# Two transformer blocks on one core: the order of the attention's steps, the two halves of a weight slab apart, and three smaller edits

## The reference

```python
# first block
mod = cond @ w_ada + b_ada                       # sh1, sc1, g1, sh2, sc2, g2, 1024 each
h = rms(x) * ln1_g * (1 + sc1) + sh1
fq, fk, fv, fg, dq, dk, dv = split(h @ w_in)
cum = cumsum(log_sigmoid(fg + b_f))              # forget gate, one per fox head and token
fox:  s = q.k / 8 + cum[t] - cum[s];  p = softmax(where(causal, s, -inf));  p @ v      # 8 heads
diff: p = softmax(q1.k1 / 8 + alibi) - lam * softmax(q2.k2 / 8 + alibi);    p @ v      # 4 heads
diff_out = rms(diff_out) * diff_norm_g * (1 - lam_init)
x = x + g1 * (concat(fox_out, diff_out) @ w_out)
h2 = rms(x) * ln2_g * (1 + sc2) + sh2
x = x + g2 * ((silu(h2 @ w_gate) * (h2 @ w_up)) @ w_down)
# second block: h @ w_in_2 (7 x 1024 columns), a spatial gating unit, 16 heads of causal attention with
# a bias by relative position, two gates, w_out_2, a squared-relu feed-forward, a per-layer gate, a last norm
```

## Time and profile before

| | us |
|---|---|
| median of 3 executions (lowest, highest) | 817.07 (816.53, 818.65) |
| the profiled execution, and its span | 818.92, 817.2 |
| PE busy | 775.0 (95%) |
| DVE busy | 466.4 (57%) |
| ACT busy | 390.6 (48%) |
| POOL busy | 59.4 (7%) |

### The profile page before, as it was taken

One profiled execution on the slowest core, in us unless ns is written; L12 is line 12 of the kernel. 1 busy time (PEld: TensorE's weight loads), 2 busy tenths in 40 slices (PEclk: granted clock), 3 DMA queues, 4 the chain that ended last, 5 costly groups with the idle time before them and its releaser, 6 DMA issues.

```text
span 817.2 us, 10224 instructions
## 1 busy us (share of the span) xinstructions
PE 775.0 (95%) x3955; PEld 616.8 (75%) x3955; DVE 466.4 (57%) x607; ACT 390.6 (48%) x544; POOL 59.4 (7%) x70
## 2 busy tenths in 40 slices
PE   3988899988999999999999999999999999999995
PEld 2667675656888889888878887777888888888884
DVE  3466676747565556464595436555565656545364
ACT  3255666644344334353634356665455545335252
POOL 2004030010000000000280000000010000000001
PEclk9999999999999999999999999999999999999998
DMA  9998336895655347656749464333565645564601
GB/s 275 289 361 274 112 105 254 312 397 195 219 194 184 125 155 232 232 180 203 255 162 331 155 205 154 105 104 111 170 194 162 200 156 201 164 201 154 206 26 51
DMA packets 86785, 158.73 MB, mean 194 GB/s; under 512 B 5226, under 2 KB 23875, under 8 KB 84690
## 3 DMA queue, kind: packets, MB, share of 16 engines
q1 hardware_dynamic: 84562, 151.16, 55.7%
q0 software_dynamic: 2128, 6.90, 2.7%
q10 hardware_dynamic: 48, 0.01, 0.0%
HBM read 156.99 MB, written 1.08 MB: 193 GB/s over the span
## 4 chain that ended last, share of the span: by engine, by line
PE 82%; DVE 5%; issue 3%; SPq 3%; ACT 3%; DMA 2%; POOL 1%; DVEq 0%; POOLq 0%; ACTq 0%
PE PS L872 25%; PE PS L874 24%; PE PS L873 24%; PE PS L986 3%; DMA raw<-in_w_ada 2%; PE PS L1066 1%; ACT whi L1165 1%; PE PS L960 1%; DVE wlo L1377 1%; PE PS L1037 1%; SPq L802 1%; PE PS L1092 1%; PE PS L1021 1%; SPq L790 1%; POOL hrs L1780 1%
## 5 line engine op out<-in xcount | busy, mean ns | idle before, releaser
L1377 DVE TENSOR_TENSOR wlo<-raw,whi 128x2048 fp32r<-128x2048 f32 (+1 forms) x126 | 280.2, 2226 | 190.4 <-ACT whi L1165 162.4
L1165 ACT ACTIVATE whi<-raw 128x2048 fp32r<-128x2048 f32 (+1 forms) x126 | 227.1, 1804 | 156.2 <-PE PS L874 156.2
L872 PE MATMUL PS<-whi,hT 128*128 128x512 f32 (+1 forms) x704 | 280.6, 399 | 2.2 <-issue 1.9
L874 PE MATMUL PS<-whi,hT 128*128 128x512 f32 (+1 forms) x704 | 272.8, 388 | 0.0
L873 PE MATMUL PS<-wlo,hT 128*128 128x512 f32 (+1 forms) x704 | 272.7, 387 | 0.0
L872 PEld LDWEIGHTS PS<-whi,hT 128*128 128x128 f32 x704 | 133.5, 190 | 33.1 <-issue 8.4
L874 PEld LDWEIGHTS PS<-whi,hT 128*128 128x128 f32 x704 | 133.3, 189 | 27.5
L873 PEld LDWEIGHTS PS<-wlo,hT 128*128 128x128 f32 x704 | 133.7, 190 | 23.9
L872 PE MATMUL PS<-whi,hidT 128*128 128x512 f32 x216 | 84.5, 391 | 0.0
L874 PE MATMUL PS<-whi,hidT 128*128 128x512 f32 x216 | 84.1, 389 | 0.0
L873 PE MATMUL PS<-wlo,hidT 128*128 128x512 f32 x216 | 84.1, 389 | 0.0
(11 more groups left out here) (227 smaller groups left out, 643.7 us busy)
## 6 DMA issues: line engine op xcount, KB each, us to landing
raw<-in_w_in SPq DMA_DIRECT2D x36, 1024.0 KB, 5.1
raw<-in_w_ff SPq DMA_DIRECT2D x32, 1024.0 KB, 5.2
raw<-in_w_ada SPq DMA_DIRECT2D x16, 1024.0 KB, 6.9
raw<-in_w_gate SPq DMA_DIRECT2D x10, 1024.0 KB, 5.4
raw<-in_w_up SPq DMA_DIRECT2D x10, 1024.0 KB, 5.1
raw<-in_w_down SPq DMA_DIRECT2D x10, 1024.0 KB, 5.2
raw<-in_w_ada SPq DMA_DIRECT2D x16, 512.0 KB, 7.2
raw<-in_w_out SPq DMA_DIRECT2D x8, 1024.0 KB, 5.1
```

The lines of the kernel that those rows point to most:

```text
L872: pe.matmul(o, ah, wh, start=(k == 0), stop=False)
L874: return pe.matmul(o, al, wh, start=False, stop=end)
L1165: act.activation(split_view(whi, i), slab_view(raw, slot, i), ACT.Copy).then_inc(hi_made, 1)
L1377: dve.tensor_tensor(split_view(wlo, i), slab_view(raw, slot, i), whole(split_view(whi, i)), ALU.subtract).then_inc(lo_made, 1)
```

## The change

1. **Row constant.** The fox heads' bias no longer has `cum[t]`: the step `cum` (two transposes, a copy) and, for each head, the two adds to `mcum` are gone; the bias is the mask alone.
2. **Attention.** `scores` is taken apart into `scores` (TensorE; maximum on VectorE), `exp` (ScalarE) and `probs` (VectorE's divisions). `heads u+2` follow right behind `scores u+1`, ahead of `exp` and `probs` of u+1.
3. **Slabs.** `split n` is now only the `whi` copy; `lower n` is the `wlo` subtraction. While pairs are worked on (`paired`), `lower` stands behind `probs`, or ahead of the slab's first piece if it has not come before; `split` stands behind `values`.
4. **Start.** `fgate` (forget gate) stands ahead of split 10, and `lam` is in two steps, the first in the start.
5. **Diff norm.** By two heads, the first two behind values 6; their turn stands ahead of `ada 18`.
6. **Norm 1.** `x` is no longer multiplied by the inverse root ahead of the transposes. VectorE makes a diagonal matrix of the inverse roots, and TensorE multiplies by it in place of the transpose (`first`, `turn`), tokens 0 to 127 first.

```diff
-BETWEEN = {"fox": (2, 1, 1, 2, 2), 1: (2, 1, 1, 2, 1), 2: (2, 1, 1, 1, 1), 3: (2, 0, 1, 1, 1),
+BETWEEN = {"fox": (3, 2, 1, 2), 1: (2, 2, 1, 2), 2: (2, 2, 1, 1), 3: (2, 1, 1, 1),
...
             if u != us[-1]:
                 out += [("scores", u + 1)]
+            if u + 2 <= us[-1]:
+                out += [("heads", u + 2)]
+            if u != us[-1]:
+                out += [("exp", u + 1), ("probs", u + 1)]
...
-            if u + 2 <= us[-1]:
-                out += [("heads", u + 2)]
...
+            if u == FOX_P + 2:
+                out += [("diffnorm", 0)]
+            if u == FOX_P + 3:
+                out += [("diffnorm", 1)] + turns("diff", 0, (0,))
...
-            order += {KC - 4: [("setup", 0)], KC - 3: early + [("relbias", 0)]}.get(j, [])
+            order += {KC - 4: [("setup", 0), ("lam", 0)], KC - 3: early + [("relbias", 0)]}.get(j, [])
...
-    order += early + [("fgate", 0), ("unit", 0), ("logf", 0), ("unit", 1)]
+    order += [("fgate", 0)] + early + [("unit", 0), ("logf", 0), ("unit", 1)]
     now = whole("fox", 2, "w_in", 2 * W, "h")
-    order += insert(now, (4, early), (5, [("cum", 0)]), (6, [("heads", 0)]))
+    order += insert(now, (4, early), (6, [("heads", 0)]))
...
         if it[0] == "piece" and it[1]["first"] and it[1]["slab"] >= KC + 2:
-            while split <= min(it[1]["slab"] + min(2, it[1]["slab"] + 1), len(slabs) - 1):
-                out.append(("split", split))
-                split += 1
+            held = tiles[it[1]["T"]]["name"] == "w_out" and it[1]["k"] == 4 and tiles[it[1]["T"]]["n"] == 1
+            split = up_to("split", split, max(wanted, it[1]["slab"] + 1))
+            wanted = it[1]["slab"] + (2 if held else 3)
+            if not paired:
+                split = up_to("split", split, wanted)
+            lower = up_to("lower", lower, it[1]["slab"] + 1 if paired else split)
         out.append(it)
+        if it[0] == "scores":
+            paired = it[1] not in (FOX_P + DIFF_P - 1, PAIRS - 1)
+        if it[0] == "probs":
+            lower = up_to("lower", lower, split)
+        if it[0] == "values":
+            split = up_to("split", split, wanted)
...
+                elif kind == "first":
...
+                    for c in range(2):
+                        k = 2 * i + c
+                        pe.matmul(PS[:, b, c * S:c * S + P], x[:, 0, k * P:(k + 1) * P], diag[:, 0, :], start=True, stop=True)
...
-                            dve.tensor_scalar(mcum[:, a % 2, 0:P], mask[:, P:2 * P], cumq[:, 0, a:a + 1], None, ALU.add)
...
-                            bias = [mcum[:, a % 2, c0:c1] for c0, c1 in QB]
+                            bias = [mask[:, P:2 * P], mask]
...
+                elif kind == "norm" and i == 1:
+                    for t in range(TB):
+                        dve.wait_ge(rs1_made, t + 1)
+                        dve.tensor_scalar(diag[:, t, :], ident, nrs[:, 1, t:t + 1], None, ALU.mult).then_inc(diag_made, 1)
```

More of the change, by code:

```diff
@@ L203, in plan @@
     tail += insert(fill, *[(j, [ada[10 + j]] + ([("grow", 0)] if j == 5 else [])) for j in range(8)])
-    order += [("scores", 0), ("heads", 1), ("lam", 0)] + tail[:3]
+    order += [("scores", 0), ("heads", 1), ("exp", 0), ("probs", 0)] + tail[:3]
     tail = tail[3:]
     order += attention(list(range(FOX_P + DIFF_P)), tail, ada[18:20])
-    order += [("diffnorm", 0)] + ada[20:21] + turns("diff", 0, (0, 1)) + ada[21:22]
-    order += slab(wo[0], "w_out", 0, 4) + [("evac", wo[0])]
+    order += ada[20:22] + turns("diff", 0, (1,)) + insert(slab(wo[0], "w_out", 0, 4), (2, [("mod", 1)])) + [("evac", wo[0])]
     order += insert(slab(wo[1], "w_out", W, 4), (1, [("sums", (1, 0))])) + [("evac", wo[1]), ("sums", (1, 1))] + ada[22:24]
-    order += [("mod", 2), ("norm", 1)]
-    order += turns("norm", 1, (0, 1)) + parts("norm", 1, (0, 1)) + turns("norm", 1, (2, 3)) + parts("norm", 1, (2, 3))
+    order += [("norm", 1), ("first", 0), ("mod", 2), ("first", 1)]
+    order += turns("norm", 1, (0, 1)) + parts("norm", 1, (0, 1)) + [("first", 2), ("first", 3)]
+    order += turns("norm", 1, (2, 3)) + [("split", None)] + parts("norm", 1, (2, 3))
     late = []
@@ L230, in plan @@
                 m = FOX_P + DIFF_P
-                now = insert(now, (0, [("heads", m)]), (3, [("scores", m), ("heads", m + 1)]))
+                now = insert(now, (0, [("heads", m)]), (3, [("scores", m), ("heads", m + 1), ("exp", m), ("probs", m)]))
             order += now
@@ L982, in _ @@
                         pe.wait_ge(s, v)
-                    for c in range(2):
-                        for t in range(TB):
-                            o = c * S + t * P
-                            last = pe.transpose(PS[:, b, o:o + P], src[:, t, c * P:(c + 1) * P], ident)
+                    if is_affine(i):
+                        for c in range(2):
+                            last = pe.matmul(PS[:, b, c * S + P:(c + 1) * S], src[:, 1, c * P:(c + 1) * P], diag[:, 1, :],
+                                             start=True, stop=True)
+                    else:
+                        for c in range(2):
+                            for t in range(TB):
+                                o = c * S + t * P
+                                last = pe.transpose(PS[:, b, o:o + P], src[:, t, c * P:(c + 1) * P], ident)
                     last.then_inc(turned, 1)
@@ L1001, in _ @@
                     reader[6] = [(cum_made, 1)]
-                elif kind == "cum":
-                    take(5)
-                    pe.wait_ge(cum_made, 1)
-                    for t in range(TB):
-                        last = pe.transpose(PS[:, 5, t * FOX:(t + 1) * FOX], fgt[0:FOX, 3, t * P:(t + 1) * P],
-                                            ident[0:FOX, 0:FOX])
-                    last.then_inc(cumq_ps, 1)
-                    reader[5] = [(cumq_in, 1)]
                 elif kind == "heads":
@@ L1371, in _ @@
                 kind, i = it
-                if kind == "split":
-                    slot = landed(dve, it)
+                if kind == "lower":
+                    slot = landed(dve, ("split", i))
                     dve.wait_ge(hi_made, i + 1)
@@ L1444, in _ @@
                     last.then_inc(lam_dot, 1)
+                elif kind == "lam":
                     dve.wait_ge(lam_exp, 1)
@@ L1811, in _ @@
                     n = i
+                    if n == 1:
+                        for t in range(TB):
+                            pool.wait_ge(sums_made, 3 + t)
+                            then(pool.tensor_tensor(nss[:, 1, t:t + 1, 0], nss[:, 1, t:t + 1, 0], nss[:, 1, t:t + 1, 1], ALU.add))
+                            last = inverse_root(nrs[:, 1, t:t + 1], nss[:, 1, t:t + 1, 0], D)
+                            last.then_inc(rs1_made, 1)
+                        continue
                     if n:
```

123 lines of the change are left out of this document (64 added, 59 removed).

## The result

The changed kernel takes **873.33 us** (median of 4 runs, 872.39 to 873.54) where the kernel before, on the same chip, takes 817.86: ratio 1.068 (1.066 to 1.070). The forecast was 847 with a range to 857. The sign and the late low halves of the first block came out as forecast; behind the first block's gate products 19.4 us more were lost than forecast, most of it in the second block's attention.

A forecast was written before the change was run, and what follows sets the result against it. TensorE, busy 775.0 of 817.2 us, was taken as the bound. Terms 4.2 + 1.9 + 4.8 + 4.4 + 9.0 + 3.3 − 1.1 + 3.6 = +30 on 818.9 gave 849, by the median 847 us; range 829 to 857.

The forecast's parts named there:

- slab 12: First block: its low half stands behind the hss reduction, so it starts 5.4 us late, plus 1.7 of slow clock.
- Slab 13: First block: its low half stands behind probs 2, so TensorE waits 4.6 us, plus 1.7 of slow clock.
- Heads 0: Start of attention: wait for the second `unit` leaves a gap of 5.75 us, with 1.7 of slow clock +7.4.
- heads 4: First block, behind scores 3: needs `unit 3`, ready at 135.2 but wanted at 132.3, +2.9 us.
- Slabs 15 and 16: First block: low halves late behind probs, +1.7 us for slab 15 and +3.05 for slab 16.
- the strict queue: SP queue: slab 18's transfer waits for lower 16 and delays `ada 11` behind it, +3.5 us and 1.7 clock.
- the sum for MoBA: Second block's attention: waits of 2.2 us go, lower 77 costs 3.85 and 1.7 clock, other low halves in time; net +3.6.
- the price of the clock: TensorE: every gap over about 2 us costs its length and 1.7 us more at half speed.
- rival 1: Stalls only: low halves late, but the clock holds or the queue is not late; 835 to 837, both 826; chance 0.24.
- norm 1: Gate: scaling and its wait go, sixteen diagonal products cost 1.7 us extra, lower 21 costs 0.5; net −1.1 us.
- the faster one: VectorE makes low halves 12, 13 and 16 in time, so only removed waits count: 17 us less, 800; chance 0.05.
- Worse: Late low halves delay later transfers further, each another 1 to 2 us through `ada` chunks: 858 to 865; chance 0.06.

The follow-up runs named there:

- back_first: The changed kernel with the second block's low halves placed behind `back` on VectorE instead of ahead of it: 854.51 us, ratio 1.046.
- heads_back: start_back with heads u+2 between the probability transposes again, as in the kernel before: 815.52 us, ratio 0.996.
- start_back: The changed kernel with both slab halves at one place, forget gate behind split 10 and `lam` behind pair 0's divisions again: 820.20 us, ratio 1.002.
- best4: heads_back with pair 0's exponentials and divisions ahead of heads 1, and heads 0 one piece later: 810.71 us, ratio 0.991.

## Why the prediction was right in one half and wrong in the other

**Right: the low half is the loss, and slab 12 decides.** "Slab 12 can start about 5.4 us after slab 11's last matmul": it was 5.20, at 104.64. Slab 13: 4.6 forecast, 4.31 measured. Heads 0: 5.75 and 5.52; heads 4: 2.9 and 2.91; ada 11: 3.5 and 3.91. Slabs 15 and 16 were over-sized: 1.7 and 3.05, measured 1.03 and 1.98. With both halves at one place (822 us) all waits for slabs and transfers are gone, and their places alone bring most of the loss into the kernel before (859.5 us), so the cause is shown.

**Right: the strict queue.** With slab 18's transfer behind it, `ada 11` waits 2.8 us less; up to the gate about 1.9 of it stay gained. All the ada waits were forecast as 8.8 us and are 10.7. The 7.1 us of the earlier trace rows was no measure of this stretch: from 155 to 210 us a transfer of ada weights takes 10.5 to land, at the median of 13.

**Wrong: the second block.** The step that failed is the sum for MoBA: "Lower 77 stands behind probs 10 … +3.85 … The other slabs' lower halves are in time: between pairs there are five pieces … +3.6 net". The 3.85 is right (3.53), and the other low halves are in time for their slabs. What was left out is what stands behind them on VectorE: `back`, on whose bank of `PS` the next `probsT` waits. The term was put at nothing; it is five waits of 2.2 to 2.6 us, 12.4 in all, and half clock behind them: from 530 to 620 us the granted clock is 0.89, where it was 1.00. From the first gate piece to the end it took 23.0 us more instead of 3.6, and back_first takes 16.1 of these away by that place alone. The rest of the miss, 3.3 us, no run parts. The trace of before had it. In this pair `back` (the first row, on VectorE) ends at 529.49 us, and the transposes (the second, on TensorE) start at 529.64, so nothing could come ahead of `back` for free:

```profile
529.07 0.42 DVE L1650 TENSOR_TENSOR tok<-PS,rinv 128x256 f32<-128x256 f32 x1
...
529.64 0.52 PE L1066 MATMUL PS<-con,sc 128*128 128x128 f32 x3
```

The prediction looked at when each low half ends, and not at who is queued behind it.

**Wrong: the price of the clock.** "A gap over about 2 us therefore costs its length and 1.7 more." The price was too small at some gaps. Behind slab 12 the clock is 0.50 not for 3.4 us but for six of work (the window from 104 to 108 above; from 108 to 110 it is 0.50 too), which costs near 3. Behind slab 13 it is 0.60 over four, which costs 1.6. And the length of the gap did not decide: from 203 to 210 us the clock is 0.53, behind three gaps of 1.72, 1.42 and 1.46 us, while in the profile of back_first, the same program up to there, gaps of 1.61, 1.49 and 1.46 at the same place are followed by a clock of 1.00. The piece of that stretch behind the mark at w_out0 makes most of the difference between the 3.0 us that this mark was off and the 4.9 of the gate; the piece ahead of it cost about 1.2. The number of falls from 75 to 170 us, "six or seven", came out (six). The sum itself holds six stretches of 1.7, not the seven that rival 1 counts.

**Luck in the marks.** They fit within 1.3 us up to scores 5 in part because errors cancel: the clock cost more than was priced, and slabs 15 and 16 together 1.7 less. Two executions of one program also differ by some of this: heads 0 start at 78.24 us here and at 77.85 in back_first.

**Wrong in size: norm 1.** The extra for sixteen products by a diagonal was taken as 1.7 us. In the changed kernel eight such products (first row) take as long as eight transposes (second row):

```profile
225.45 1.06 PE L1017 MATMUL PS<-diag,x 128*128 128x128 f32 x8
...
254.48 1.03 PE L1023 MATMUL PS<-con,hid 128*128 128x128 f32 x8
```

The extra is 0, but for weight loads of 192 ns instead of 140, which run beside the products. From the end of w_out1 to the gate it was 7.9 us, forecast 7.7: a wait of 1.1 for `diag` came instead. The total fits by luck. The Trainium skill ("Perfetto Trace Analysis", Optimizing Tensor Performance, Transposes) says to do a logical transpose as a transpose and not as a standard matmul. By these rows the standard matmul costs TensorE nothing here, at 128 columns in float32.

**The rivals.** The stalls-only case (835 to 837) and the faster one fell. "Worse" (858 to 865) was the nearest. Its reason, further delay of the `ada` transfers, is there but small (10.7 us for 8.8); the loss lies elsewhere.

## What to carry to other kernels

Before a step is put ahead of others on an engine, list what comes to stand behind it up to the next wait of the bounding engine, and for each of those the buffer or bank that it frees. A low half may be in time itself and late for its neighbour: here a step of 2.3 us, in five pairs, on an engine that was idle for up to 7 us right after, cost 16 us. Place long preparatory work behind the short step that others wait for, and keep it well ahead of its own use; if a strict transfer queue waits for it too, count the transfers behind.

## What the runs showed of the hardware that was not expected

The half-speed level of TensorE's clock (granted 0.50, 1.2 GHz) does not follow from the length of the gap before it: 3.23 us was followed by full speed and 3.26 by half speed in two executions of one program, and three gaps of 1.4 to 1.7 us in a row were followed by 0.53 over seven us in one execution and by 1.00 in another. Times of one kernel go with its clock: the two runs of heads_back at 812.9 and 813.3 us have a granted clock of 0.996 over the span, the five from 815.3 to 816.1 one of 0.990 to 0.991. start_back ran from 816.9 to 822.5 us, best4, whose gaps behind 60 us are all under 2 us, from 810.4 to 811.3. And a float32 product of 128 by 128 by 128 took the time of a transpose of that size, 0.11 us from start to start.
